# High parts first in every product, three gathered products per head, and the gate table stored in halves

## The reference, cut to what matters

```python
def peer(h, p):
    q = jnp.einsum('nd,dq->nq', x, p['w_query']).reshape(n, PK_HEADS, 2, HALF_KEY)
    s1 = jnp.einsum('nhc,hkc->nhk', q[:, :, 0], p['sub_keys'][0])
    s2 = jnp.einsum('nhc,hkc->nhk', q[:, :, 1], p['sub_keys'][1])
    v1, i1 = lax.top_k(s1, TOPK)
    v2, i2 = lax.top_k(s2, TOPK)
    cand = (v1[..., :, None] + v2[..., None, :]).reshape(n, PK_HEADS, TOPK * TOPK)
    cidx = (i1[..., :, None] * N_KEYS + i2[..., None, :]).reshape(n, PK_HEADS, TOPK * TOPK)
    top_s, pos = lax.top_k(cand, TOPK)
    idx = jnp.take_along_axis(cidx, pos, axis=-1)
    gates = jax.nn.softmax(top_s.astype(F32), axis=-1).astype(h.dtype)
    ...
        act = jax.nn.gelu(jnp.einsum('nd,nhkd->nhk', xb, eu[ib]))
        return jnp.einsum('nhk,nhkd->nd', act * gb, ev[ib])
```

## Time and profile before

| | us |
|---|---|
| median of 3 runs | 2963.63 |
| lowest and highest run | 2952.79, 2965.68 |
| the profiled execution | 2947.76 |
| its span | 2946.0 |
| heads, from the first split of tokens to the first wide product | 1254 to 1547.5 |
| scatter | 1547.5 to 1978 |
| rest | 1978 to 2203 |
| down and the tail | 2203 to 2946 |

### The profile page before, as it was taken

One profiled execution on the slowest core, in us unless ns is written; L12 is line 12 of the kernel. 1 busy time (PEld: TensorE's weight loads), 2 busy tenths in 40 slices (PEclk: granted clock), 3 DMA queues, 4 the chain that ended last, 5 costly groups with the idle time before them and its releaser, 6 DMA issues.

```text
span 2946.0 us, 59339 instructions
## 1 busy us (share of the span) xinstructions
PE 2808.8 (95%) x24142; PEld 2472.4 (84%) x24142; DVE 2182.4 (74%) x3103; ACT 1220.8 (41%) x1889; POOL 922.8 (31%) x624
## 2 busy tenths in 40 slices
PE   6999999999999999899999999999999999999998
PEld 4999998677777869799998888888887778788776
DVE  3246553665666553579989999988888999899998
...
GB/s 405 266 117 128 128 128 78 143 135 120 138 146 151 133 103 128 72 207 236 197 250 371 374 399 398 392 398 414 417 403 418 418 418 418 416 418 418 418 418 310
DMA packets 205969, 813.60 MB, mean 276 GB/s; under 512 B 81328, under 2 KB 99888, under 8 KB 116688
## 3 DMA queue, kind: packets, MB, share of 16 engines
...
...
## 4 chain that ended last, share of the span: by engine, by line
PE 28%; DMA 13%; DVE 9%; issue 4%; POOL 1%; ACT 1%; SPq 1%; another core or an unknown queue 0%; DVEq 0%; ACTq 0%
DMA work<-act_table 12%; PE ps L2017 10%; PE ps L2018 5%; DVE work L2684 2%; DVE x L2563 2%; DVE wlo L2689 1%; DVE wlo L1984 1%; PE ps L2307 1%; PE ps L2308 1%; PE ps L2309 1%; PE ps L2009 1%; PE ps L2010 1%; PE ps L2011 1%; PE ps L2412 1%; PE ps L2414 1%
## 5 line engine op out<-in xcount | busy, mean ns | idle before, releaser
L2017 PE MATMUL ps<-hboth,whi 128*128 128x512 f32 x1664 | 588.3, 398 | 11.1 <-DVE wlo L1984 11.1
L2018 PE MATMUL ps<-hboth,wlo 128*128 128x256 f32 x1664 | 463.3, 278 | 0.0
L2451 POOL DMA_INDIRECT work<-expert_v,idx x128 | 297.8, 2326 | 420.4 <-DVE work L2684 403.8
L2412 PE MATMUL ps<-whi,hboth 128*128 128x512 f32 x1024 | 402.3, 393 | 22.6 <-DVE wlo L2689 19.9
L2413 PE MATMUL ps<-wlo,hboth 128*128 128x512 f32 x1024 | 399.7, 390 | 0.0
L2414 PE MATMUL ps<-whi,hboth 128*128 128x512 f32 x1024 | 399.7, 390 | 0.0
L2017 PEld LDWEIGHTS ps<-hboth,whi 128*128 128x128 f32 x1664 | 312.2, 188 | 83.7 <-DVE wlo L1984 13.2
L2451 POOL DMA_INDIRECT x<-u_rows,idx x128 | 235.4, 1839 | 429.4 <-DVE x L2563 247.4
L2018 PEld LDWEIGHTS ps<-hboth,wlo 128*128 128x128 f32 x1664 | 313.4, 188 | 0.0
L2684 DVE SCALAR_TENSOR_TENSOR work<-work,dots 128x2048 f32<-128x2048 f32 x127 | 297.9, 2346 | 0.6 <-DMA work<-expert_v,idx 0.5
L2412 PEld LDWEIGHTS ps<-whi,hboth 128*128 128x128 f32 x1024 | 192.9, 188 | 71.1 <-DVE wlo L2689 29.0
...
## 6 DMA issues: line engine op xcount, KB each, us to landing
...
z<-w_ada SPq DMA_DIRECT2D x32, 1024.0 KB, 11.4
...
```

Source lines behind the costliest of these rows:

```text
L2017: pe.matmul(both, whi[:, r, k, :], hboth[:, :, k, CTX:T], start=(k == 0), stop=False)
L2018: last = pe.matmul(both[:, 0], wlo[:, r, k, :], hhi[:, k, CTX:T], start=False, stop=(k == KD - 1))
L2412: pe.matmul(bank, ah, vh[:, part], start=first, stop=False)
L2451: nc.gpsimd.indirect_dma_start(out=buf, out_offset=None, in_=rows, in_offset=bass.IndirectOffsetOnAxis(ap=idx[:, s:s + 1], axis=0)).then_i ...
```

## The change

1. **High parts first.** In query and up products all matmuls with `whi` come first, and only then those with `wlo`; PE waits for the low part before the second group and not at the start. The wide products and the down products are cut in the same way. The matmuls are the same, in another order.
2. **Three gathered products per head.** `EARLY_DOTS` goes from 14 to 21, in the scatter stage 67 are left (two per round, and three in 3 of the 32 rounds). The indices of the second 16 slots are made after `choose(1)`. POOL starts three gathers per head.
3. **Two stores per set of the gate table**, by halves of the keys: the first half where the whole set was stored, the second after the first product of the next round; the last one in the second product of the rest stage, whose first turn is written out for that on ACT. The waits count 32 per set instead of 16.

```diff
@@ -1841,9 +1841,11 @@
         U_PRE = PKH * UPH
         U_SCAT = U_PRE + UPRE
         U_REST = U_SCAT + USCAT
-        EARLY_DOTS = 2 * (PKH - 1)
-        SCAT_DOTS = [3 if i % 3 == 2 else 2 for i in range(SCAT)]
-        assert EARLY_DOTS + sum(SCAT_DOTS) + REST == SLOTS and EARLY_DOTS <= TOPK
+        DOTS_PER_HEAD = 3
+        EARLY_DOTS = DOTS_PER_HEAD * (PKH - 1)
+        IN_SCAT = SLOTS - REST - EARLY_DOTS
+        SCAT_DOTS = [IN_SCAT * (i + 1) // SCAT - IN_SCAT * i // SCAT for i in range(SCAT)]
+        assert EARLY_DOTS + sum(SCAT_DOTS) + REST == SLOTS and EARLY_DOTS <= 2 * TOPK
         TURN_OF = 12
         TURNS = (REST - 4) // TURN_OF
         assert REST == TURNS * TURN_OF + 4 and M_SCAT % 2 == 0 and M_REST % 2 == 0
@@ -2000,21 +2002,29 @@
         def rest_of_low(pe, m):
             pe.wait_ge(w_low[m % 2].sem, m // 2 + 1)
 
-        def up_product(pe, m, bank):
+        def high_first(pe, m, bank, tokens):
             r = m % 2
+            pe.wait_ge(front_high.sem, front_high.v + m - 1)
+            for k in range(KD):
+                if k == FRONT_K:
+                    pe.wait_ge(w_high.sem, m + 1)
+                pe.matmul(bank, whi[:, r, k, :], hhi[:, k, tokens], start=(k == 0), stop=False)
+                pe.matmul(bank, whi[:, r, k, :], hlo[:, k, tokens], start=False, stop=False)
+            front_of_low(pe, m)
             for k in range(KD):
                 if k == FRONT_K:
                     rest_of_low(pe, m)
-                moving_hi, moving_lo = hhi[:, k, CTX:T], hlo[:, k, CTX:T]
-                pe.matmul(bank, whi[:, r, k, :], moving_hi, start=(k == 0), stop=False)
-                pe.matmul(bank, whi[:, r, k, :], moving_lo, start=False, stop=False)
-                last = pe.matmul(bank, wlo[:, r, k, :], moving_hi, start=False, stop=(k == KD - 1))
+                last = pe.matmul(bank, wlo[:, r, k, :], hhi[:, k, tokens], start=False, stop=(k == KD - 1))
             last.then_inc(prod.sem, 1)
 
-        def wide_product(pe, r, bank):
+        def wide_high(pe, r, bank):
             both = bank.rearrange("p (s t) -> p s t", s=2)
             for k in range(KD):
                 pe.matmul(both, whi[:, r, k, :], hboth[:, :, k, CTX:T], start=(k == 0), stop=False)
+
+        def wide_low(pe, r, bank):
+            both = bank.rearrange("p (s t) -> p s t", s=2)
+            for k in range(KD):
                 last = pe.matmul(both[:, 0], wlo[:, r, k, :], hhi[:, k, CTX:T], start=False, stop=(k == KD - 1))
             last.then_inc(prod.sem, 1)
 
@@ -2081,7 +2091,7 @@
                         spill(m - 4 - NQ)
                 load_fixed(M_DOWN - 1)
                 for r in range(2):
-                    sp.wait_ge(stage_out[r].sem, 16 * (SETS // 2))
+                    sp.wait_ge(stage_out[r].sem, 32 * (SETS // 2))
                     sp.wait_ge(spilled[r].sem, 16 * 2)
                 groups(0, 0)
                 load_v(expert_v[0], 0)
@@ -2170,14 +2180,15 @@
                     s, t0 = q // 16, (q % 16) * 4
                     act.wait_ge(table_done.sem, q + 1)
                     if q % 16 == 0 and s >= 2:
-                        act.wait_ge(stage_out[s % 2].sem, 16 * (s // 2))
+                        act.wait_ge(stage_out[s % 2].sem, 32 * (s // 2))
                     nc.scalar.activation(stage[:, s % 2, :, t0:t0 + 4],
                                          ps[:, (0, 1, 4, 5)[q % 4], :].rearrange("p (t i) -> p i t", t=4),
                                          ACT.Copy).then_inc(staged.sem, 1)
 
-                def store_set(s):
+                def store_half(s, half):
+                    keys = slice(half * NK // 2, (half + 1) * NK // 2)
                     act.wait_ge(staged.sem, GT // 4 * (s + 1))
-                    act.dma_start(gate_table[:, 0:NK, s * GT:(s + 1) * GT], stage[:, s % 2]).then_inc(stage_out[s % 2].sem, 16)
+                    act.dma_start(gate_table[:, keys, s * GT:(s + 1) * GT], stage[:, s % 2, keys]).then_inc(stage_out[s % 2].sem, 16)
 
                 for n in range(UPRE):
                     gelu(M_PRE + n, U_PRE + n)
@@ -2198,6 +2209,8 @@
                     keep_half(0, 2 * i)
                     high_of(act, m + 2)
                     gelu_sum(g)
+                    if q and q % (GT // 4) == 0:
+                        store_half(q // (GT // 4) - 1, 1)
                     copies(q + 1)
                     if i < SCAT - 1:
                         gate_quad(q + 3)
@@ -2205,10 +2218,12 @@
                     high_of(act, m + 3)
                     gelu_sum(g + 1)
                     if (q + QUADS) % (GT // 4) == 0:
-                        store_set(q // (GT // 4))
+                        store_half(q // (GT // 4), 0)
 
                 def rest(it, n):
                     r = n % 2
+                    if isinstance(it, int) and (it, n) == (0, 1):
+                        store_half(SETS - 1, 1)
                     keep_half(it, USCAT + n)
                     if isinstance(it, int) and it * TURN_OF + n >= REST - 2:
                         act.wait_ge(v_landed[r].sem, 16)
@@ -2221,7 +2236,9 @@
                     out = act_of(it * TURN_OF + (U_REST + n), r)
                     nc.scalar.activation(out, out, ACT.Gelu_apprx_tanh).then_inc(u_out.sem, 1)
 
-                with act.Fori(0, TURNS - 1) as it:
+                for n in range(TURN_OF):
+                    rest(0, n)
+                with act.Fori(1, TURNS - 1) as it:
                     for n in range(TURN_OF):
                         rest(it, n)
                 for n in range(TURN_OF):
@@ -2297,25 +2314,15 @@
                                 last.then_inc(prod.sem, 1)
 
                 def query(m, i):
-                    r, u = m % 2, i % 2
-                    front_of_low(pe, m)
                     pe.wait_ge(q_out.sem, i - 1)
-                    bank = ps[:, u, 0:T]
-                    for k in range(KD):
-                        if k == FRONT_K:
-                            rest_of_low(pe, m)
-                        pe.matmul(bank, whi[:, r, k, :], hhi[:, k, :], start=(k == 0), stop=False)
-                        pe.matmul(bank, whi[:, r, k, :], hlo[:, k, :], start=False, stop=False)
-                        last = pe.matmul(bank, wlo[:, r, k, :], hhi[:, k, :], start=False, stop=(k == KD - 1))
-                    last.then_inc(prod.sem, 1)
+                    high_first(pe, m, ps[:, i % 2, 0:T], slice(0, T))
 
                 def up(m, g):
-                    front_of_low(pe, m)
                     if g == 1:
                         pe.wait_ge(ht_out.sem, 4)
                     if g >= 2:
                         pe.wait_ge(u_out.sem, g - 1)
-                    up_product(pe, m, ps[:, 2 + g % 2, 0:LAT])
+                    high_first(pe, m, ps[:, 2 + g % 2, 0:LAT], slice(CTX, T))
 
                 def turn_tokens(j):
                     if j >= 2:
@@ -2373,12 +2380,14 @@
                     last.then_inc(table_done.sem, 1)
 
                 def wide_up(m, g):
-                    pe.wait_ge(w_low[m % 2].sem, m // 2 + 1)
+                    pe.wait_ge(w_high.sem, m + 1)
                     if g - 2 >= U_SCAT:
                         pe.wait_ge(up_summed.sem, up_summed.v + g - 1 - U_SCAT)
                     else:
                         pe.wait_ge(u_out.sem, g - 1)
-                    wide_product(pe, m % 2, ps[:, 2 + g % 2, :])
+                    wide_high(pe, m % 2, ps[:, 2 + g % 2, :])
+                    pe.wait_ge(w_low[m % 2].sem, m // 2 + 1)
+                    wide_low(pe, m % 2, ps[:, 2 + g % 2, :])
 
                 for i in range(SCAT):
                     m, g, q = M_SCAT + 2 * i, U_SCAT + 2 * i, QUADS * i
@@ -2390,14 +2399,16 @@
                 with pe.Fori(0, REST // 4) as it:
                     for n in range(4):
                         r = n % 2
+                        pe.wait_ge(w_high.sem, it * 4 + (M_REST + n + 1))
+                        pe.wait_ge(up_summed.sem, it * 4 + (up_summed.v + USCAT + n - 1))
+                        wide_high(pe, r, ps[:, 2 + r, :])
                         pe.wait_ge(w_low[r].sem, it * 2 + (M_REST // 2 + n // 2 + 1))
-                        pe.wait_ge(up_summed.sem, it * 4 + (up_summed.v + USCAT + n - 1))
-                        wide_product(pe, r, ps[:, 2 + r, :])
+                        wide_low(pe, r, ps[:, 2 + r, :])
 
                 def down(it, b, first=False, last=False):
 
                     r = b % 2
-                    pe.wait_ge(w_low[r].sem, it * 2 + (M_DOWN // 2 + b // 2 + 1))
+                    pe.wait_ge(w_high.sem, it * 4 + (M_DOWN + b + 1))
                     if r == 0:
                         pe.wait_ge(act_split.sem, it * 2 + (b // 2 + 1))
                     vh, vl = [t[:, r].rearrange("p k c -> p (k c)") for t in (whi, wlo)]
@@ -2410,8 +2421,13 @@
                             if first and tile == 0 and c >= 2:
                                 pe.wait_ge(up_summed.sem, up_summed.v + NK - U_SCAT - 3 + c)
```

(29 more changed lines are left out.)

## The result

The changed kernel takes 2984.66 us, the median of 5 runs (2984.17 to 2986.53), where the kernel before takes 2961.17 (5 runs, 2952.79 to 2965.68): a ratio of 1.0114, with a 95% interval of 1.0088 to 1.0139. It is slower by 1.1%, and lies outside the forecast range of 2944 to 2976. The profiled execution took 2984.62 us, with a span of 2982.8, 36.8 more than before.

What follows compares the result with a forecast made beforehand. PE was taken to bound the head, scatter and rest stages and DMA the down stage. Terms -14.1 + 7.7 + 3.0 = -3.4 us gave 2944.4, scaled to 2960 us, range 2944 to 2976.

Steps and rivals of the forecast that it cites:

- What bounds the stages: PE sets the pace in the head, scatter and rest stages, with DVE level or close; DMA binds the down stage.
- Part 1: Scatter stage: high parts first ends PE's waits for low parts after third dots, 12.98 us for all 32 rounds, -14.1 us.
- Part 2: Head stage: seven more dots make DVE late, gates done at 1548.0 instead of 1534.3, +7.7 us.
- The stall of some 2 us: Head stage: PE waits for a late low part in one of the last 8 ups, some 2 us at most.
- The clock: At the transposes: PE stands some 6 us, then works six us at half the clock, +3.0 us, from 0 to 5.
- Part 3: Gate table stores in halves: they land just in time and four more ACT issues fit in idle time, 0 us.
- Part 4: Down products: high first takes most of PE's 18.7 us low-part waits away, but DMA is late next, 0 (0 to -19).
- The sum: Whole kernel: -14.1 + 7.7 + 3.0 = -3.4 us on the profiled 2947.8, so 2944.4, scaled to 2960 us.
- the down stage gains: Rival: 418 GB/s is only what is asked for in the down stage, -22 us, so 2938; chance 0.09.
- DVE stays late: Rival: every head-stage dot meets a POOL half block, gates at 1574, PE stands 33 us, +22, so 2986; chance 0.11.
- The stage is not free: Rival: the store halves land late, 5 us for each of two sets, +10, so 2970; chance 0.08.
- a copy of ACT that waits for a store: Listed sign that the forecast is wrong: an ACT copy held up by a gate table store; no size given.

## Why the prediction was wrong, point by point

- **What bounds the stages: right.** With whole stores PE is busy 414.9 of 414.9 us in the scatter stage and the down stage is at 418 GB/s in each of the twelve kernels (2260 to 2900 us).
- **Part 1, -14.1: right in size; the mechanism holds, but not alone.** Copies in undisturbed stretches are 6.48 us apart with no 7.85 as in the earlier trace rows. With whole stores the stage is 14.6 us shorter by ACT's copies. DVE works 391 us in it instead of the 407 in the earlier trace rows. But the forecast put all of it down to the order of the matmuls. Three dots per head with the old order gives 6.1 us of it, and the new order with two dots 2.6, as a store then stands: the gain needs the gathers that part 2 moves out.
- **Part 2, the heads: right in the main.** The dots by head, from the lengths below and their like, are 12.2, 13.0, 11.3, 8.4, 7.4, 7.2 and 11.7 us; stepped were 13.0, 13.4, 11.4, 8.1, 7.5, 7.4 and 10.2, both 71 in sum. The timelines of PE (its first product of the stage, before), of DVE (one dot each of heads 1 to 3), of POOL (the first gather for head 4) and of PE (the transposes), and the window of 5 us around the last:

```profile
1252.50 0.69 PE L2310 MATMUL ps<-hboth,whi 128*128 128x384 f32 x1 [6.78 <-DVE hboth L362]
...
1336.35 3.26 DVE L2579 SCALAR_TENSOR_TENSOR x<-x,htok 128x2048 f32<-128x2048 f32 x1 [0.25 <-DVEq L2565]
...
1374.68 4.48 DVE L2579 SCALAR_TENSOR_TENSOR x<-x,htok 128x2048 f32<-128x2048 f32 x1
...
1408.04 4.49 DVE L2579 SCALAR_TENSOR_TENSOR x<-x,htok 128x2048 f32<-128x2048 f32 x1
...
1443.97 2.23 POOL L2467 DMA_INDIRECT x<-u_rows,idx  x1 [2.96 <-DVE x L2579]
...
1545.11 0.69 PE L2365 MATMUL ps<-tab,gates 128*128 128x128 f32 x2 [5.96 <-DVE gates L2604]
```

```profile
1545.00:1550.00 5.00, 4.89 (x23) 4.89 (x24) 4.72 (x6) 2.09 (x5) 4.04 (x3) 0.50 0.85 288
```

  The dots have the price of the earlier trace rows beside POOL, POOL waits from head 4 on, and PE waits 5.96 us for the gates, until 1545.11 where 1548.0 was forecast. Of the 2.9 us between, 1.7 were there before the stage began (1252.50 for 1254.20). The stall of some 2 us allowed for the last 8 ups came as two, 1.9 and 1.1 us.
- **The clock, +3.0: right within its range of 0 to 5.** From the transposes to the first quad PE took 9.1 us instead of 6.4, +2.7, at a clock of 0.50. In the kernel with whole stores the same stand of 5.96 us cost only 1.4 (7.8 us; the clock was back to 0.73 in the same 5 us), so the 2.7 so near 3.0 is in part luck. Here the forecast took a stand of 6 us, where its own sum had 7.7. With part 2 the heads are 9.2 us longer from the start of the stage, and 10.7 was forecast.
- **Part 3, 0: wrong, and the whole miss.** The step that failed is "Four more issues on ACT of 0.4 us lie in its idle time of 2 us per product". The issues of the four second halves take 17.4 to 18.0 us and cost PE 47.2 us. 0.4 us was read from the earlier trace rows, four issues of which none had more than a few hundred unsent runs ahead of it. The most had the fourth; ACT's queue in the kernel before, from the issue of the third store to that of the fourth, shows 16157 of 16384 runs sent:

```profile
q10 hardware_dynamic: 16157, 4.13, 17.1%
```

  So an issue behind a DMA with thousands of unsent runs was not in the trace, and its price should have been bounded by the rows at hand. The nearest is the landing of 103.3 us for 16384 runs, thus some 52 for half of them, less the 6.5 until the second issue: an estimate of 0 to some 45 us of ACT standing per set. The range would then have held the result. The step looked only at when the bytes land. That landing was no trouble in the changed kernel: the halves land 24.8 to 29.5 us after their issue, the last one 60.5. What the step allowed up to 7 us for, a wait for the last store at the end of the rest stage, came with whole stores: the loads that wait for its landing start 12.1 us ahead of the last copy of the rest stage, and PE stands 4.6 us for them (2.5 us before).
- **Part 4, 0: right in number, wrong on the waits.** Little time changed there (743.8 for 747.9), as DMA sets the pace. But "high first takes most of them away" did not come: PE still waits 16.4 us for low parts (19 times), where it was 18.7. In the down stage ACT's waits, once 408.8 us for PE, are now mostly for loads:

```profile
ACT whi L2266 <- DMA raw<-expert_v: 132.6, 55, 3.3
ACT whi L2266 <- DMA work<-expert_v: 127.0, 51, 3.6
```

  The 4 us that it is shorter by go with the last store: SP's first load for the down stage waits for its landing. In the eight kernels whose stores stood this load starts 18.6 to 23.2 us ahead of the last copy of the rest stage, and the down stage takes 743.3 to 744.6 us. In the kernel before and in the one with whole stores and three dots throughout it starts 12.7 and 12.1 us ahead, and the stage takes 747.8 in both; the other two kernels lie between. No experiment changed this alone.
- **The sum.** Its other terms gave -3.4 us; the changed kernel with whole stores measured -5.7 between the medians. With 47.2 in place of the 0, it is 2944.4 + 47.2 = 2991.6 for an execution that took 2984.6; the rest is the 4 us of the down stage and smaller parts. One slip in the rivals: with -22 us "the down stage gains" comes to 2941 and not 2938, which changes no chance.
- **The rivals.** None had this mechanism. "DVE stays late" has almost the measured time, 2986, and that is luck: it asked for gates at 1574 and a PE that stands 33 us at the transposes, and these came at 1545.11 after 5.96 us. "The stage is not free" looked at the same stores and priced their landing at 10 us. The last line of the forecast named "a copy of ACT that waits for a store" as a sign against it, and that is near to what came: a copy that waits behind the store's issue.
